# A mixer and mixture-of-experts layer on one core: the order of the weight loads, and which engine scales the transposed tokens

## The chip, the cores and the metric

The kernel runs on one core of a Trainium2 chip. The metric is the device time of one execution in microseconds (us), as the median of three runs. All arithmetic is float32. TensorE (PE in the profile) multiplies matrices, VectorE (DVE), ScalarE (ACT) and GpSimd (POOL) work on rows of 128 partitions, and SyncE (SP) issues nearly all loads in the order of one program of its own, here called the SP queue.

## What is computed

One layer for 256 latent tokens and 256 context tokens of width 1024, cut to what matters here:

```python
mod_x = silu(c) @ w_mod + b_mod            # w_mod (1024, 6144): shift1, scale1, gate1, shift2, scale2, gate2
hx = modulate(rmsnorm(x, g_mix), x_sh1, x_sc1)      # the same for the context, with c_ctx
ux = hx @ w_in; uc = hc @ w_in[:, POOL_W:]
ssm_x = ssm_output(ux_ssm, scans...)       # two directions, 32 groups of 64 complex states, GELU, sigmoid GLU
pool_x = pool_mixer(ux[..., :POOL_W], w_pool, s_pool)
x = x + x_g1 * (concatenate([pool_x, ssm_x]) @ w_out)
hx2 = modulate(rmsnorm(x, g_ffn), x_sh2, x_sc2)
eidx, gate = route(hx2, w_router, b_router)         # 2 of 32 experts for each token
for each expert e:                         # w_gate, w_up (1024, 512), w_down (512, 1024)
    y += gate * ((silu(h @ w_gate[e]) * (h @ w_up[e])) @ w_down[e])
return rmsnorm(x + x_g2 * y, g_final)
```

## The kernel before

The program of each engine is written out by hand, with semaphores between them; nothing reorders it. A load of 128 x 2048 float32 is 1 MiB; w_mod comes as 24 such chunks, a third (8 chunks, k = 0 to 7) for each pair of the six vectors.

**The head.** Tokens are normalised by ScalarE and transposed by TensorE (L456), four 128 x 128 pieces for each k of the 8 column blocks, into two PSUM banks in turn. Whoever empties a bank applies scale and shift in the same step and writes hT: ScalarE for even k (L851), VectorE for odd k (L1112, in `modulate_tokens`, which `powers_times` calls in the middle of its last products for SA). TensorE may fill a bank again when it has been emptied (semaphores `ht_ready`, `ht_ready_dve`). Behind it come the second half of the transposes of SA (L435, `turn_sa`), the projection u (L484, L491), the states' matmuls (L528), and VectorE's scans, which end with `hp_ready`.

The last third of w_mod isn't multiplied on TensorE: VectorE sums its chunks, weighted, into `acc` (`mod_sum`, L1237 and L1240), chunks 0 to 2 right behind the scans, 3 to 5 behind `ysum` (L1251), 6 and 7 behind the products that fill `cat` (L1257, printed as L999, the line of the helper `tt`). The chunks go through three buffers; the SP queue asks for chunk k of this third when VectorE has counted up `mod2_used` to k - 2. `y_mm` tells that L591 is done, `mix_pool` that the pooling part of the output projection is. TensorE's L610 is the matmul of the GLU, ScalarE's L916 its sigmoid, L621 the second part of the output projection, four blocks of four matmuls; before its third block stands L628, which turns `acc` into a column and waits for all eight chunks (`mod2_used`).

**The expert rounds.** Eight rounds (`four`) of four experts j = 0 to 3. For each expert TensorE multiplies gate and up side by side (`gate_up`, L728 and L729), each in two halves of k, 2 MiB a half, and counts `gu_half` behind each half. There are two buffers for gate and up, b = j % 2, and four for down, one for each expert. Behind the four experts and the adding of the round before (`scatter`, L702) come the down matmuls of all four experts, side by side in four column groups (`down`, L761), again in two halves; `down_half` is counted after the first half, `down_mm` at the end. Then `gather` (L696) lays out the tokens of the next round. The SP queue asks for a half when its buffer is free: `second_two(i)` loads gate and up of j = 2, 3 of round i, `downs(i)` the down matrices of round i, `next_two(i)` gate and up of j = 0, 1 of round i + 1. Round 0's down matrices are loaded in the head.

TensorE matmuls of float32 are two instructions each in the profile, transposes one.

The functions that the diff touches follow, with the lines of the profile.

Of the kernel before, what the change touches and what calls it, by code (L numbers as in the profile page):

```python
# [6 lines left out]
ALU = mybir.AluOpType  # L7
# [50 lines left out]
def hybrid_block(nc, x, ctx, w_mod, columns, ssm_bc, b_mod_rows, w_in, w_out, w_pool, w_glu, w_router, b_router,  # L58
                 w_gate, w_up, w_down, g_final, consts, pool_consts, out):
    D = x.shape[2]  # L60
    KD = D // P
    T = x.shape[1]
    NT = T // P
    NE = w_router.shape[1]
# [8 lines left out]
    with ExitStack() as stack:  # L73
# [164 lines left out]
        def _(sp):  # L238
# [53 lines left out]

            sp.wait_ge(S("mix_pool"), 1)
            sp.wait_ge(S("hp_ready"), 1)
            gu_load(sp, 0, 0, 0, "up")
            gu_load(sp, 0, 0, 1, "up")
            for half in range(2):
                down_load(sp, lambda j: j, half, (0, 1))

# [3 lines left out]
            for k in range(3, KD):  # L303
                mod_chunk(2, k)
            sp.wait_ge(S("mod2_used"), KD)
# [17 lines left out]
            def downs(i):  # L323

                sp.wait_ge(S("down_half"), i)
                down_load(sp, lambda j: (4 * i + j) % NE, 0)
                sp.wait_ge(S("down_mm"), 4 * i)
                down_load(sp, lambda j: (4 * i + j) % NE, 1)
# [12 lines left out]
            with sp.Fori(1, last_four) as i:  # L341
                second_two(i)
                downs(i)
                next_two(i)
            second_two(last_four)
            downs(last_four)
            for t in range(2 * NT):
                sp.wait_ge(S("fin_ready"), t + 1)
                tt, h = t // 2, t % 2
# [52 lines left out]
        def _(pe):  # L402
# [22 lines left out]
            def turn_sa(d, r):  # L425

                pe.wait_ge(S("sa_ready"), 2 * d + r + 1)
                for g4 in range(4):
                    n = 8 * d + 4 * r + g4
                    if n in (8, 9):  # L430
                        pe.wait_ge(S("ht_ready_dve" if n % 2 else "ht_ready"), KD)
                    elif n >= 2:
                        pe.wait_ge(S("st_copy"), n - 1)
                    for g in range(4):
                        mm = pe.transpose(ps[:, (n + 1) % 2, 128 * g:128 * g + 128],  # L435
                                          SA[:, d, r, 4 * g4 + g].rearrange("p s j -> p (s j)"), ident)
                    mm.then_inc(S("sa_t"), 1)
# [12 lines left out]
            for k in range(KD):  # L450
                if k == 1:
                    pe.wait_ge(S("mod_col"), 1)
                elif k >= 2:
                    pe.wait_ge(S("ht_ready_dve" if k % 2 else "ht_ready"), 2 * (k // 2))
                for t in range(4):
                    mm = pe.transpose(ps[:, (k + 1) % 2, 128 * t:128 * t + 128], xc[:, t, P * k:P * k + P], ident)  # L456
                mm.then_inc(S("x_t"), 1)
# [37 lines left out]
            pe.wait_ge(S("ht_ready"), KD)  # L495
            pe.wait_ge(S("ht_ready_dve"), KD)
# [306 lines left out]
        def _(act):  # L803
# [44 lines left out]
            for k in range(0, KD, 2):  # L848
# [140 lines left out]
        def _(dve):  # L989
# [85 lines left out]
            def powers_times(dst, pw, m, r, sign_im, done, between=None):  # L1075

                for d in range(2):
                    for rr in r:
                        for h in range(2):
                            if between and (d, rr, h) == (1, 1, 1):  # L1080
                                between()
# [24 lines left out]
            def modulate_tokens():  # L1106

                dve.wait_ge(S("a1_ready"), 1)
                for k in range(1, KD, 2):
                    dve.wait_ge(S("x_t"), k + 1)  # L1110
                    for q in (1, 0):
                        dve.tensor_scalar(hT[:, k, 256 * (1 - q):256 * (2 - q)], ps[:, (k + 1) % 2, 256 * (1 - q):256 * (2 - q)],  # L1112
                                          A1[:, k, q:q + 1], MC[:, 0, k, q:q + 1], ALU.mult, ALU.add).then_inc(S("ht_ready_dve"), 1)

            powers_times(SA, PW, Br, (0, 1), 1, "sa_ready", modulate_tokens)


# [341 lines left out]
```

## Time and profile before

| | |
|---|---|
| median of three runs | 716.72 us (716.46 to 719.92) |
| profiled execution, its own time | 720.47 us |
| its span, first to last instruction | 718.7 us |
| mean granted TensorE clock | 0.943 |
| busy: PE, DVE, ACT, POOL | 602.8, 217.3, 144.3, 23.8 us |
| loaded by the SP queue (q1) | 244.98 MB |
| mean rate of all loads | 344 GB/s |

Times of the trace are microseconds from the first instruction. In the page's rows a digit or a number stands for a fortieth of the span. A row of the windows gives the stretch, its length, the busy time of PE, PEld (TensorE's weight loads), DVE, ACT and POOL with the number of instructions in brackets, the mean granted TensorE clock (1.00 is 2.4 GHz, 0.50 is 1.2 GHz), the busy share of the 16 DMA engines and the rate in GB/s. A row of the chain of waits gives start, duration, and what was worked on or waited for; a row of the timeline gives start, duration, engine, line, operation, written tile <- read tiles, their sizes, and in brackets how long the engine was idle before and what ended that. SPq is the SP queue issuing a load; the load itself runs later. The name "ra" covers the tokens, hT and the expert inputs, "rc" the last two down buffers and SA, "wts" the weight buffers and cat, "r" is the third w_mod buffer.

### The profile page before, as it was taken

The numbers are of one execution on the slowest core, as the hardware profiler recorded it, in microseconds if no ns is written. First come the engines' busy times: TensorE is split into PE (matmuls) and PEld (weight loads), VectorE is DVE, ScalarE is ACT, GpSimd is POOL, SyncE is SP. The second block draws the span as 40 slices with busy tenths as digits, with TensorE's granted clock in tenths as the row PEclk, the third lists the DMA queues.
The fourth block names the chain that finished last, engine by engine and source line by source line (L and its number), as shares of the span: only waits on it lengthen the run. The fifth ranks groups of instructions, "written<-read, shape, count | busy, mean of one in ns | idle before, by whom it ended". The sixth has DMA issues, their size and how long they took to land.

```text
span 718.7 us, 9339 instructions
## 1 busy us (share of the span) xinstructions
PE 602.8 (84%) x3784; PEld 259.8 (36%) x3784; DVE 217.3 (30%) x494; ACT 144.3 (20%) x224; POOL 23.8 (3%) x31
## 2 busy tenths in 40 slices
PE   4658997887496999997998898899799889889875
PEld 0236436445242433432433333243343333334221
DVE  7974974992756200200200200010020020010003
ACT  3632014203011221221221221022122112102011
POOL 1800000000000000000000000000000000000000
PEclk9778999996798999999999999999999999999998
DMA  8981447789647699399999999999999999999981
GB/s 343 407 322 30 133 76 231 247 340 420 262 176 310 255 423 387 138 425 423 420 423 423 421 422 422 422 421 421 423 421 423 422 422 422 422 422 420 421 342 58
DMA packets 44078, 247.26 MB, mean 344 GB/s; under 512 B 8356, under 2 KB 10036, under 8 KB 16280
## 3 DMA queue, kind: packets, MB, share of 16 engines
q1 hardware_dynamic: 39592, 244.98, 84.4%
q10 hardware_dynamic: 4160, 1.05, 0.6%
q0 software_dynamic: 304, 0.93, 0.4%
q8 instruction: 15, 0.25, 0.1%
q14 instruction: 7, 0.06, 0.0%
HBM read 242.75 MB, written 2.10 MB: 341 GB/s over the span
## 4 chain that ended last, share of the span: by engine, by line
PE 34%; DMA 31%; SPq 6%; DVE 4%; issue 2%; ACT 1%; POOL 0%; DVEq 0%; ACTq 0%; POOLq 0%
DMA rc<-in_w_down 26%; PE ps L728 16%; PE ps L761 10%; SPq L233 5%; PE ps L696 4%; DMA wts<-in_w_mod 3%; DMA wts<-in_w_up 2%; PE ps L621 1%; SPq L226 1%; PE ps L702 1%; PE ps L591 1%; DVE ra L999 1%; DVE cb L999 0%; DVE rc L999 0%; DVE ra L1276 0%
## 5 line engine op out<-in xcount | busy, mean ns | idle before, releaser
L728 PE MATMUL ps<-wts,ra 128*64 128x512 f32 x512 | 227.0, 595 | 17.7 <-DMA wts<-in_w_up 16.3
L729 PE MATMUL ps<-wts,ra 128*64 128x512 f32 x512 | 227.2, 596 | 0.0
L761 PE MATMUL ps<-wts,ra 128*32 128x512 f32 x512 | 119.3, 621 | 31.0 <-DMA rc<-in_w_down 31.0
L728 PEld LDWEIGHTS ps<-wts,ra 128*64 128x64 f32 x512 | 67.2, 137 | 156.4 <-issue 126.6
L761 PE MATMUL ps<-rc,ra 128*32 128x512 f32 x512 | 119.3, 622 | 0.0
L999 DVE TENSOR_TENSOR ra<-ra,ps 128x256 f32<-128x256 f32 x32 | 13.5, 421 | 264.7 <-ACT ra L956 264.6
L950 ACT COPY ra<-ps 128x512 f32<-128x512 f32 x32 | 33.6, 1050 | 199.7 <-PE ps L729 199.7
L761 PEld LDWEIGHTS ps<-wts,ra 128*32 128x32 f32 x512 | 32.5, 114 | 109.2 <-issue 83.5
L729 PEld LDWEIGHTS ps<-wts,ra 128*64 128x64 f32 x512 | 67.2, 137 | 0.0
L999 DVE TENSOR_TENSOR cb<-ps,ra 128x512 f32<-128x512 f32 x32 | 22.1, 692 | 142.9 <-PE ps L761 142.9
L945 ACT COPY ra<-ps 128x512 f32<-128x512 f32 x32 | 18.4, 587 | 148.8 <-PE ps L696 141.9
L696 PE MATMUL ps<-cb,ra 128*128 128x128 f32 x256 | 32.6, 288 | 1.5 <-issue 1.2
L696 PEld LDWEIGHTS ps<-cb,ra 128*128 128x128 f32 x256 | 30.9, 201 | 7.6 <-DVE cb L999 5.9
L702 PE MATMUL ps<-cb 128*128 128x512 f32 x68 | 32.9, 606 | 0.0
L761 PEld LDWEIGHTS ps<-rc,ra 128*32 128x32 f32 x512 | 29.6, 114 | 0.0
L484 PE MATMUL ps<-ra,wts 128*128 128x512 f32 x64 | 29.1, 608 | 0.0
L621 PE MATMUL ps<-wts 128*128 128x512 f32 x32 | 17.4, 703 | 9.0 <-DVE wts L999 9.0
L414 PE MATMUL ps<-wts,sil 128*32 128x512 f32 x88 | 15.2, 770 | 8.9 <-DMA wts<-in_w_mod 8.9
L739 PEld LDWEIGHTS ps<-cst,ra 128*128 128x128 f32 x128 | 14.2, 140 | 17.2 <-issue 15.3
L999 DVE TENSOR_TENSOR ps<-pws,cb 128x1024 f32<-128x1024 f32 x16 | 20.2, 1264 | 0.0
L398 POOL TENSOR_TENSOR small<-small 128x1 f32<-128x1 f32 x4 | 2.2, 555 | 538.4 <-DVE small L1406 496.1
L999 DVE TENSOR_TENSOR rc<-pws,cb 128x1024 f32<-128x1024 f32 x16 | 19.6, 1224 | 0.6
(218 smaller groups left out, 515.9 us busy)
## 6 DMA issues: line engine op xcount, KB each, us to landing
wts<-in_w_up SPq DMA_DIRECT2D x64, 1024.0 KB, 13.2
wts<-in_w_gate SPq DMA_DIRECT2D x64, 1024.0 KB, 11.1
wts<-in_w_down SPq DMA_DIRECT2D x32, 1024.0 KB, 18.2
rc<-in_w_down SPq DMA_DIRECT2D x32, 1024.0 KB, 22.3
wts<-in_w_mod SPq DMA_DIRECT2D x16, 1024.0 KB, 10.0
r<-in_w_mod SPq DMA_DIRECT2D x8, 1024.0 KB, 11.2
wts<-in_w_in SPq DMA_DIRECT2D x2, 2048.0 KB, 14.0
wts<-in_w_out SPq DMA_DIRECT2D x2, 2048.0 KB, 10.4
```

Of the source, the lines that this page charges most:

```text
L233: eng.dma_start(Wd[j].rearrange("p k d -> p (k d)")[:, at], w_down[0, four(j)].rearrange("(p k) d -> p (k d)", k=FC)[:, at]).then_inc(S(f" ...
L414: mm = pe.matmul(ps[32 * j:32 * j + 32, bank, :], silc[:, k, :], wm[n % 3][:, 512 * j:512 * j + 512], start=False, stop=(k == KD - 1))
L484: mm = pe.matmul(ps[:, 4 + q % 3, :], WB[:, k, 512 + P * q:512 + P * q + P], hT[:, k, :], start=(k == 0), stop=(k == KD - 1))
L621: mm = pe.matmul(ps[:, n, :], cat[:, 4 + k, P * (n // 2):P * (n // 2) + P], wo_ssm[:, k, 512 * (n % 2):512 * (n % 2) + 512], start=False, ...
L696: mm = pe.matmul(o, h2P[:, t, k, :], Pm[:, t], start=True, stop=True, skip_group_check=True)
L702: mm = pe.matmul(ps[:, 2 * t + h, :], PT[:, t, :], oS[:, 2 * h + t, :], start=False, stop=stop, skip_group_check=True)
L728: pe.matmul(ps[0:64, 4 + b, :], st, Wg[b][:, k, :], start=(k == 0), stop=(k == KD - 1))
L729: mm = pe.matmul(ps[64:128, 4 + b, :], st, Wu[b][:, k, :], start=(k == 0), stop=(k == KD - 1))
L761: mm = pe.matmul(ps[32 * j:32 * j + 32, BANKS[n], :], hid[:, j, f, SLOTS * t:SLOTS * t + SLOTS], Wd[j][:, f, 512 * h:512 * h + 512], start ...
L945: act.copy(xm[:, 2 * r:2 * r + 2], ps[:, BANKS[r], :].rearrange("p (k e s) -> p k e s", k=2, e=4)).then_inc(S("xm_ready"), 1)
L950: act.copy(gu[:, j % 2, :].rearrange("p (f q) -> p q f", f=FC), ps[:, 4 + j % 2, :].rearrange("p (q f) -> p q f", f=FC)).then_inc(S("gu_co ...
L999: return dve.tensor_tensor(o, a, b, op)
```

## The change

The SP queue's order changes at two places. In the head, chunks 3 to 5 of w_mod's last third move ahead of everything else, the x rows ahead of the two up loads, and the down loads of experts 0 and 1 behind chunks 6 and 7. In the rounds, `downs` is split into halves, and both are asked for ahead of `second_two(i)`; in the last round only the first half is, and the second one stays behind. And ScalarE scales all eight k of the transposed tokens; VectorE's part of it and the semaphore `ht_ready_dve` are gone, so that `ht_ready` counts to 16.

```diff
--- before.py
+++ after.py
@@ -290,18 +290,19 @@
             for k in range(3):
                 mod_chunk(2, k)
 
+            for k in range(3, 6):
+                mod_chunk(2, k)
             sp.wait_ge(S("mix_pool"), 1)
             sp.wait_ge(S("hp_ready"), 1)
-            gu_load(sp, 0, 0, 0, "up")
-            gu_load(sp, 0, 0, 1, "up")
-            for half in range(2):
-                down_load(sp, lambda j: j, half, (0, 1))
-
             sp.wait_ge(S("y_mm"), 1)
             for t in range(NT):
                 sp.dma_start(x2[:, t, :], x[0, t * P:(t + 1) * P]).then_inc(S(f"xres_in{t}"), 16)
-            for k in range(3, KD):
+            gu_load(sp, 0, 0, 0, "up")
+            gu_load(sp, 0, 0, 1, "up")
+            for k in range(6, KD):
                 mod_chunk(2, k)
+            for half in range(2):
+                down_load(sp, lambda j: j, half, (0, 1))
             sp.wait_ge(S("mod2_used"), KD)
             gu_load(sp, 0, 0, 0, "gate")
             gu_load(sp, 0, 0, 1, "gate")
@@ -320,12 +321,10 @@
                         sp.wait_ge(S("gu_half"), 8 * i + 2 * b + half + 1)
                         gu_load(sp, b, (4 * i + 2 + b) % NE, half)
 
-            def downs(i):
-
-                sp.wait_ge(S("down_half"), i)
-                down_load(sp, lambda j: (4 * i + j) % NE, 0)
-                sp.wait_ge(S("down_mm"), 4 * i)
-                down_load(sp, lambda j: (4 * i + j) % NE, 1)
+            def downs(i, half):
+
+                sp.wait_ge(S("down_mm" if half else "down_half"), 4 * i if half else i)
+                down_load(sp, lambda j: (4 * i + j) % NE, half)
 
             def next_two(i):
 
@@ -339,11 +338,13 @@
             sp.wait_ge(S("passes_ready"), 1)
             last_four = sp.value_load(pairs[0:1, 0:1], min_val=NE // 4 - 1, max_val=NE - 1)
             with sp.Fori(1, last_four) as i:
+                downs(i, 0)
+                downs(i, 1)
                 second_two(i)
-                downs(i)
                 next_two(i)
+            downs(last_four, 0)
             second_two(last_four)
-            downs(last_four)
+            downs(last_four, 1)
             for t in range(2 * NT):
                 sp.wait_ge(S("fin_ready"), t + 1)
                 tt, h = t // 2, t % 2
@@ -428,7 +429,7 @@
                 for g4 in range(4):
                     n = 8 * d + 4 * r + g4
                     if n in (8, 9):
-                        pe.wait_ge(S("ht_ready_dve" if n % 2 else "ht_ready"), KD)
+                        pe.wait_ge(S("ht_ready"), 2 * KD)
                     elif n >= 2:
                         pe.wait_ge(S("st_copy"), n - 1)
                     for g in range(4):
@@ -451,7 +452,7 @@
                 if k == 1:
                     pe.wait_ge(S("mod_col"), 1)
                 elif k >= 2:
-                    pe.wait_ge(S("ht_ready_dve" if k % 2 else "ht_ready"), 2 * (k // 2))
+                    pe.wait_ge(S("ht_ready"), 2 * (k - 1))
                 for t in range(4):
                     mm = pe.transpose(ps[:, (k + 1) % 2, 128 * t:128 * t + 128], xc[:, t, P * k:P * k + P], ident)
                 mm.then_inc(S("x_t"), 1)
@@ -492,8 +493,7 @@
                                    start=(k == 0), stop=(k == KD - 1))
                 mm.then_inc(S("u_pool_mm"), 1)
 
-            pe.wait_ge(S("ht_ready"), KD)
-            pe.wait_ge(S("ht_ready_dve"), KD)
+            pe.wait_ge(S("ht_ready"), 2 * KD)
             pe.wait_ge(S("win_ssm_in"), 16)
             turn_sa(1, 0)
             u_ssm(0)
@@ -845,7 +845,7 @@
             mod_columns(0, 0)
 
             act.wait_ge(S("a1_ready"), 1)
-            for k in range(0, KD, 2):
+            for k in range(KD):
                 act.wait_ge(S("x_t"), k + 1)
                 for q in (1, 0):
                     act.activation(hT[:, k, 256 * (1 - q):256 * (2 - q)], ps[:, (k + 1) % 2, 256 * (1 - q):256 * (2 - q)],
@@ -1072,13 +1072,11 @@
                 link(tt(bi_, bi_, u, ALU.add))
             dve.sem_inc(S("bbar_ready"), 1)
 
-            def powers_times(dst, pw, m, r, sign_im, done, between=None):
+            def powers_times(dst, pw, m, r, sign_im, done):
 
                 for d in range(2):
                     for rr in r:
                         for h in range(2):
-                            if between and (d, rr, h) == (1, 1, 1):
-                                between()
                             g = slice(8 * h, 8 * h + 8)
                             pr = pw[:, d, 0, g].unsqueeze(3).broadcast_to([P, 8, L, SG])
                             pi = pw[:, d, 1, g].unsqueeze(3).broadcast_to([P, 8, L, SG])
@@ -1103,16 +1101,7 @@
                         ins.then_inc(S(done), 1)
                         dve.wait_ge(S(done), 2 * d + rr + 1)
 
-            def modulate_tokens():
-
-                dve.wait_ge(S("a1_ready"), 1)
-                for k in range(1, KD, 2):
-                    dve.wait_ge(S("x_t"), k + 1)
-                    for q in (1, 0):
-                        dve.tensor_scalar(hT[:, k, 256 * (1 - q):256 * (2 - q)], ps[:, (k + 1) % 2, 256 * (1 - q):256 * (2 - q)],
-                                          A1[:, k, q:q + 1], MC[:, 0, k, q:q + 1], ALU.mult, ALU.add).then_inc(S("ht_ready_dve"), 1)
-
-            powers_times(SA, PW, Br, (0, 1), 1, "sa_ready", modulate_tokens)
+            powers_times(SA, PW, Br, (0, 1), 1, "sa_ready")
 
 
             dve.wait_ge(S("x_t"), KD)
```

The rows of the SP queue in the head, from behind the third chunk of w_mod's last third. wts and r<-in_w_mod are its chunks, rc<-in_x the x rows, L226 and L233 the lines that load gate or up, and down. Before:

```order
L226 DMA wts<-in_w_up 128x2048 [waits hp_ready,mix_pool]
L226 DMA wts<-in_w_up 128x2048
L233 DMA wts<-in_w_down 128x2048 x4
L302 DMA rc<-in_x 128x1024 [waits y_mm]
L302 DMA rc<-in_x 128x1024
L252 DMA wts<-in_w_mod 128x2048 [waits mod2_used]
L252 DMA r<-in_w_mod 128x2048 [waits mod2_used]
L252 DMA wts<-in_w_mod 128x2048 [waits mod2_used] x2
L252 DMA r<-in_w_mod 128x2048 [waits mod2_used]
```

And now:

```order
L252 DMA wts<-in_w_mod 128x2048 [waits mod2_used]
L252 DMA r<-in_w_mod 128x2048 [waits mod2_used]
L252 DMA wts<-in_w_mod 128x2048 [waits mod2_used]
L299 DMA rc<-in_x 128x1024 [waits y_mm,hp_ready,mix_pool]
L299 DMA rc<-in_x 128x1024
L226 DMA wts<-in_w_up 128x2048 x2
L252 DMA wts<-in_w_mod 128x2048 [waits mod2_used]
L252 DMA r<-in_w_mod 128x2048 [waits mod2_used]
L233 DMA wts<-in_w_down 128x2048 x4
```

Three of the five chunks stand ahead of all expert weights, the other two behind the up loads and ahead of the down loads.

The same queue from the start of its loop over the rounds 1 to 6 (the branch). Before, the loop starts with the gate and up loads of `second_two`:

```order
L341 UNCONDITIONAL_BRANCH
L341 ISA
L226 ISA [waits gu_half]
L226 DMA wts<-in_w_gate 128x2048
L226 DMA wts<-in_w_up 128x2048
L320 REGISTER_ALU
L226 ISA [waits gu_half]
L226 DMA wts<-in_w_gate 128x2048
L226 DMA wts<-in_w_up 128x2048
```

And now with the down loads:

```order
L340 UNCONDITIONAL_BRANCH
L233 ISA [waits down_half]
L233 DMA wts<-in_w_down 128x2048
L233 ISA
L233 DMA wts<-in_w_down 128x2048
L233 ISA
L233 DMA rc<-in_w_down 128x2048
L233 ISA
L233 DMA rc<-in_w_down 128x2048
L233 ISA [waits down_mm]
```

The second half of the down loads, with its wait for `down_mm`, follows there, and only then the eight loads of `second_two`.

## Rows read from the trace of the kernel before

**Rows 1.** Page, part 2: GB/s moved in 40 slices of 17.97 us.

```profile
GB/s 343 407 322 30 133 76 231 247 340 420 262 176 310 255 423 387 138 425 423 420 423 423 421 422 422 422 421 421 423 421 423 422 422 422 422 422 420 421 342 58
```

**Rows 2.** Windows: us, busy us per engine, TensorE clock, DMA share, GB/s.

```profile
265.00:286.00 21.00, 19.78 (x136) 7.08 (x136) 0.84 (x2) 2.18 (x4) 0.00 (x0) 1.00 1.01 418
286.00:299.50 13.50, 13.50 (x102) 6.61 (x92) 3.86 (x7) 3.62 (x5) 0.00 (x0) 1.00 0.07 16
299.50:399.50 100.00, 89.43 (x508) 33.49 (x504) 7.24 (x15) 18.09 (x25) 0.00 (x0) 0.98 1.01 421
599.50:697.30 97.80, 85.40 (x496) 32.36 (x492) 6.90 (x14) 14.27 (x23) 0.00 (x0) 1.00 1.01 420
```

**Rows 3.** Chain of waits, its last links: start us, us, what.

```profile
672.32 26.89 DMA rc<-in_w_down
699.25 8.51 PE ps L761 x64
```

**Rows 4.** Chain of waits between 160 and 205 us.

```profile
167.03 20.75 DMA wts<-in_w_mod
...
190.84 10.17 PE ps L621 x16
```

**Rows 5.** Timeline 158 to 198 us: start, us, engine, line, tiles, idle before.

```profile
158.80 0.80 SPq L226 DMA_DIRECT2D wts<-in_w_up  x2
158.82 1.29 DVE L1237 TENSOR_SCALAR cb<-wts,sil 128x2048 f32<-128x2048 f32 x1
159.65 2.35 SPq L233 DMA_DIRECT2D wts<-in_w_down  x4
...
166.08 0.43 SPq L252 DMA_DIRECT2D wts<-in_w_mod  x1
...
171.07 1.66 DVE L1251 SCALAR_TENSOR_TENSOR rc<-ut,vt,ps 128x256 f32<-128x256 f32 x4 [6.02 <-PE ps L601]
...
181.00 1.70 ACT L916 ACTIVATE rc<-ps,vt 128x256 f32<-128x256 f32 x4 [6.53 <-PE ps L610]
182.87 2.35 DVE L1240 SCALAR_TENSOR_TENSOR cb<-wts,sil,cb 128x2048 f32<-128x2048 f32 x1 [10.15 <-DMA wts<-in_w_mod]
...
190.08 2.02 DVE L999 TENSOR_TENSOR wts<-rc 128x256 f32<-128x256 f32 x4
```

**Rows 6.** Timeline 39 to 56 us, the transposed tokens.

```profile
39.70 1.02 ACT L851 ACTIVATE ra<-ps,mcol,aux 128x256 f32<-128x256 f32 x2 [1.36 <-POOL aux L382]
...
44.26 0.99 DVE L1112 TENSOR_SCALAR ra<-ps,aux,mcol 128x256 f32<-128x256 f32 x2
...
49.73 1.12 PE L456 MATMUL ps<-cst,ra 128*128 128x128 f32 x4 [0.22 <-DVE ra L1112]
...
51.98 3.78 PE L435 MATMUL ps<-cst,rc 128*128 128x128 f32 x16 [1.14 <-DVE ra L1112]
```

**Rows 7.** Windows around the transposes of rows 6, columns as in rows 2.

```profile
47.50:50.00 2.50, 2.26 (x10) 1.70 (x11) 1.00 (x2) 1.29 (x3) 0.00 (x0) 0.50 0.98 410
...
55.50:58.00 2.50, 2.50 (x6) 1.11 (x5) 2.33 (x20) 0.62 (x2) 0.76 (x1) 0.68 0.33 84
```

**Rows 8.** Chain of waits, 235 to 300 us: TensorE through the first round.

```profile
240.94 0.64 PE ps L728
...
268.08 0.64 PE ps L728
...
276.46 13.87 PE ps L761 x128
290.33 3.77 PE ps L696 x32
```

**Rows 9.** Timeline of the SP queue, 290 to 300 us.

```profile
297.95 0.35 SPq L226 DMA_DIRECT2D wts<-in_w_gate  x1
```

**Rows 10.** Windows of the third round, columns as in rows 2.

```profile
337.50:340.00 2.50, 0.03 (x3) 0.00 (x0) 0.00 (x0) 0.00 (x0) 0.00 (x0) 1.00 1.01 419
340.00:342.50 2.50, 2.20 (x12) 0.61 (x16) 0.00 (x0) 0.00 (x0) 0.00 (x0) 0.58 1.01 419
...
377.50:380.00 2.50, 1.31 (x7) 0.17 (x3) 0.00 (x0) 0.00 (x0) 0.00 (x0) 1.00 1.02 423
```

## Prediction

> **What bounds the kernel now.** I read the rate of the loads first. From slice 18 on they move 420 to 425 GB/s in every slice [rows 1], and the windows show the same 421 GB/s over 100 us at a stretch [rows 2]: the expert rounds are bound by the loads. One round loads 24 MiB (four experts of three 2 MiB matrices), 25.2 MB, so it lasts 59.8 us at 421 GB/s, while TensorE needs less: in the first round, with its matrices mostly there, it goes from 240.94 us to 294.10 us (290.33 + 3.77), 53.2 us [rows 8]. What the time is made of is then the head until the round starts, any hole in the stream of loads, and the tail behind the last byte.
>
> There is one hole in the expert rounds: 16 GB/s between 286.0 and 299.5 us [rows 2]. The first round asks for 16 MiB of gate and up matrices and then nothing, because the SP queue first wants the second round's gate and up matrices, for which TensorE must have used the first ones of that round. It does that from 294.10 us, and the request comes at 297.95 us [rows 8, 9]. The stream is full again at 299.5, so a request takes 1.5 us to reach the wires.
>
> The tail is 1.95 us from the last byte (697.3 us, [rows 2]) to the matmul that waited for it (699.25 us), and 8.51 us of the last 64 down matmuls [rows 3].
>
> In the head, the chain of waits has 20.75 us of a w_mod load and then the output projection on TensorE, L621 [rows 4]. The timeline says why: two up loads and four down loads, 6 MiB, are asked for at 158.80 us, and the fourth w_mod chunk of the last third only at 166.08 us, behind them; VectorE is idle for 10.15 us and sums it at 182.87. The products for the output projection stand behind three such sums on VectorE: they start at 190.08, though their sigmoids exist from about 181.5 us [rows 5].
>
> **The tokens, ScalarE alone.** Now VectorE comes late to its first column (44.26 us, it was in the middle of the SA products), and TensorE's transposes end so that the next step starts at 51.98 us [rows 6]. ScalarE alone does one k in 1.02 us (two halves), so eight end 8.16 us after 39.70, at 47.9, if the transposes keep up with two PSUM banks. At the lower clock four of them take 1.12 us [rows 6]; with about 0.1 us of hand-over on top of 1.02 + 1.12, a pair of k takes 2.25 us instead of 2.04, and six k so add 0.6 us. L435 starts at 48.6: **3.4 us earlier**. VectorE loses its eight scalings, 4 x 1.0 us, and the waits between them, and is ready earlier than it is wanted. ScalarE's own queue holds only the copies of the transposed SA behind this, which wait for TensorE anyway. Everything up to 158 us hangs on TensorE and then on VectorE's scans, so I carry the 3.4 us on whole.
>
> One thing can make it more. The clock was at half (0.50, its 1.2 GHz level) from 47.5 to 50 us although TensorE was busy 2.26 of 2.50 us with transposes, and it rose only in the window from 55.5, where the matmuls of u begin [rows 7]. So I keep it at half for the longer run of transposes as well. If it stayed at full, the hand-over would cost nothing (0.6), L435's 3.78 us would be 1.9 shorter at most, and this term 5.9 at most. The Trainium skill (TensorE: Matmul & The Clock Gate, Part 4: PE-mode transpose) says that a transpose does not count as work for the clock gate; by that rule the term is 3.4, which is what I sum, and by busy time alone it would be up to 5.9.
>
> **w_mod ahead of the expert weights.** Chunks 3, 4 and 5 are asked for as soon as VectorE has used chunks 0, 1 and 2, at about 160, 163 and 165 us of the old time, on a nearly empty queue. Each is 2.5 us of stream; so they are there before VectorE is through with ysum at 172.7 (171.07 + 1.66). Three sums of 2.35 us plus the gaps then end at 180.1, before the first sigmoid is done at 181.5. The products start there instead of at 190.08: **8.5 us earlier** [rows 5]. What is moved behind: the x rows, asked for after chunk 5 (about where they were), the two up loads, then chunks 6 and 7, which wait for the fourth and fifth sum (175.1 and 177.6). Ahead of chunk 6 stand chunks 3 to 5, 1 MiB of x and 2 MiB of up; that ends at 176.6, so chunk 7 is through at 181.6 and lands near 183.6. The sums 6 and 7 run after the products, from 183.6 to 188.4. TensorE wants them after eight matmuls of L621 (16 passes), started at 182.3. So they are just in time. The down loads of experts 0 and 1 end about 192 us and are needed 80 us later: nothing.
>
> L621's 16 passes took 10.17 us [rows 4] behind 9 us in which TensorE waited. Now they follow L610 within 1 us. In the rounds a pass takes 0.43 us at full clock (13.87 us for 32 steps of four matmuls side by side, [rows 8]), so 7.0 us: **3.2 us**. The first round so starts 3.4 + 8.5 + 3.2 = 15.1 us earlier, at 225.8.
>
> **Down matrices first.** The first half of the next round's down matrices is asked for when TensorE is half through this round's down matmuls: 276.46 + 6.9 = 283.4 us [rows 8], 2.6 us before the stream ran dry at 286.0. With 1.5 us to reach the wires there are 1.1 us to spare, and the hole closes: **13.5 us**.
>
> Then each round. Let F be the last byte of a round's gate and up matrices. TensorE starts on it 1.95 us later, is at the down matmuls 8.4 us after that (268.08 to 276.46), half through after another 6.9 [rows 8], and the request reaches the wires at F + 18.8. Meanwhile the queue holds the next 8 MiB, to F + 19.9. That is again 1.1 us to spare. Behind it all is loose: the second half is asked for at F + 24.2 and due at F + 28.4, the gate and up matrices at F + 31.8 and due at F + 38.3. So the waits added to the SP queue hold nothing up. For ragged hand-overs I take 0.2 us at each of seven requests, **1.4 us lost**; the ends are 0, and 2 us each, if the request comes 3 us later than I worked out.
>
> **The tail.** In the last round the second half of the down matrices comes last, behind the gate and up matrices. The queue holds 8 MiB and the first half, to F + 29.9. The next load needs TensorE to have used the first gate and up half of the last round: 1.95 + 8.4 + 13.87 + 3.77 + 3.85 (294.10 to 297.95) = F + 31.8, on the wires at F + 33.3: a new hole of 3.4 us. 8 MiB end at F + 53.2, and TensorE then does the last gate and up half, the turns and all 128 down matmuls: 1.95 + 8.4 + 13.87 = 24.2, F + 77.4. The old order would end at F + 59.8 + 1.95 + 8.51 = F + 70.2. **7.2 us lost**.
>
> **Sum.** 15.1 + 13.5 - 1.4 - 7.2 = 20.0 us. The profiled execution took 720.47 us, so it becomes 700.5; the median of the runs is 3.75 us lower than that execution, 716.72, and becomes **696.7 us**.
>
> **Rivals.** (1) *The down request comes too late in every round.* It has 1.1 us to spare and decides the stream. Landing by landing the matmuls ahead of it (L728, L702, L739) may wait for the last gate and up half a little longer. At 1 to 2 us lost in each of seven rounds, the time is 702 to 709. For it: the small margin. Against it: the first round's durations come from one trace without a gap on TensorE.
> (2) *The sums 6 and 7 are late.* They have under 1 us against TensorE's wait before L628. If chunk 7 lands 5 us later, the time is 702. Against it: nothing but 7 MiB is ahead of it after 160 us.
> (3) *Slower: the clock.* TensorE now idles before the third expert of each round, from F + 42 to F + 46.7, and a wait of under 3 us was enough to put the clock at 0.58 in the next 2.5 us [rows 10]. The four halves that follow are paced by loads of 5.0 us and cost it 3.4 us each, or 6.9 at half clock. If the clock stayed low through them and through the first half of the down matmuls, the request would come 6.9 us later, 5.8 us past the end of the queue, seven times: 41 us, so 737. It decides from 4.2 us of delay a round on (3.1 us times 7 eat the gain). Against it: with TensorE busy 1.31 of 2.50 us, in waits of the same kind, the clock stayed at 1.00 [rows 10].
> The Trainium skill (TensorE: Matmul & The Clock Gate, HAM oscillation) describes kernels that fall back to half clock at each wait for a load; by that rule this rival would hold in every round.
>
> **Chances.** Forecast 0.72, rival 1 0.14, rival 2 0.08, rival 3 0.06. A difference of 0.5%, 3.6 us, is about what a measurement of this kernel can tell. The first three are faster by more than that; of the third rival I count 0.02 as no change and 0.04 as slower. Faster 0.94. For the range: the lower end takes the full clock at the transposes (2.5), no ragged hand-overs (1.4) and a smaller tail (the new hole of 3.4 may close), down to 690; the upper end takes in most of rival 1 and rival 2, 706. Rival 3 and the rest of rival 1 are left out.
>
> **What would show it.** L851 sixteen times without VectorE's L1112, and L435 at 48 to 49 us; the products of L621 right behind the sigmoids; the first L728 near 226 us; no window under 400 GB/s from there to about 650; a DMA hole of some 3 us in the last round; from the last gate and up load 24 us to the end of the down matmuls, which wait for nothing. I am wrong if the stream has a hole in each round, if TensorE's clock is under 1.00 in the down matmuls, or if the first round starts later than 230 us.

## The result and the profile after

The changed kernel takes 696.92 us (median of 4 runs, 695.08 to 700.18), the kernel before in the same comparison 716.59 us (715.38 to 719.92): ratio 0.9712, 95% interval 0.9687 to 0.9737. In a second comparison, run for this study, it took 697.21 against 716.56 us, ratio 0.9737 (0.9708 to 0.9766). The forecast was 696.7 us, 20.0 us less; measured are 19.7 and 19.4 us less.

The profiled execution of the changed kernel took 696.92 us, exactly its median, with a span of 694.9 us; the one before had 720.47 and 718.7. From profile to profile the span is 23.8 us shorter, 4 us more than from median to median. Where these 4 us come from, as far as the runs tell, is part of what follows.

The rate of all loads after the change, in 40 slices of 17.37 us; the 138 of [rows 1] is gone, and a 342 has appeared in slice 37:

```profile
GB/s 342 384 395 32 140 108 262 238 309 394 421 277 241 344 422 421 423 422 420 423 422 422 420 423 422 422 422 423 421 420 421 422 421 423 423 421 342 423 243 61
```

Windows of the profile after, columns as in [rows 2]:

```profile
248.00:268.00 20.00, 18.77 (x124) 6.75 (x124) 0.84 (x2) 2.19 (x4) 0.00 (x0) 1.00 1.01 421
268.00:288.00 20.00, 20.00 (x136) 8.77 (x130) 3.86 (x7) 4.70 (x6) 0.00 (x0) 1.00 1.01 421
...
308.00:636.00 328.00, 299.50 (x1778) 114.81 (x1776) 32.10 (x63) 58.71 (x83) 0.00 (x0) 0.96 1.01 422
636.00:640.50 4.50, 4.50 (x24) 1.46 (x22) 0.00 (x0) 0.00 (x0) 0.00 (x0) 1.00 0.44 137
```

The stream runs at 421 to 422 GB/s through the place where the hole of 13.5 us was, and up to 636 us. The new hole, 4.5 us at 137 GB/s, is in the last round; at 422 GB/s it is worth 3.0 us. Its end, in the chain of waits after, which answers to [rows 3]:

```profile
649.89 11.84 DMA wts<-in_w_up
...
670.15 13.87 PE ps L761 x128
```

The last gate and up load lands at 661.73 us, and TensorE needs 22.3 us from there to the end of all 128 down matmuls at 684.02. The chain counts a load up to its landing, and that is later than its last byte: in [rows 3] the last down load lands at 699.21 us (672.32 + 26.89), 1.9 us behind the last byte at 697.3. From the last byte it is therefore about 24.2 us.

The head, timeline of the profile after, which answers to [rows 5] (L1226 and L1229 are VectorE's sums, L436, L485 and so on the lines that were one lower before):

```profile
151.88 5.17 PEld L591 LDWEIGHTS ps<-rc,ra 64*32 64x32 f32 x256 [4.01 <-DVE ra L999]
...
153.24 0.33 SPq L252 DMA_DIRECT2D wts<-in_w_mod  x1
...
165.68 2.35 DVE L1229 SCALAR_TENSOR_TENSOR cb<-wts,sil,cb 128x2048 f32<-128x2048 f32 x1
...
170.59 2.35 DVE L1229 SCALAR_TENSOR_TENSOR cb<-wts,sil,cb 128x2048 f32<-128x2048 f32 x1
...
174.27 1.70 ACT L916 ACTIVATE rc<-ps,vt 128x256 f32<-128x256 f32 x4 [6.75 <-PE ps L610]
174.78 2.02 DVE L999 TENSOR_TENSOR wts<-rc 128x256 f32<-128x256 f32 x4 [1.84 <-ACT rc L916]
...
175.55 7.11 PE L621 MATMUL ps<-wts 128*128 128x512 f32 x16 [0.45 <-DVE wts L999]
...
182.49 1.84 PE L628 MATMUL ps<-cst,cb 128*128 128x1 f32 x16
```

The w_mod chunk that was asked for at 166.08 us is asked for at 153.24, as soon as VectorE, through with its scans, has summed chunk 0 (151.93 to 153.22). Sum 3 runs at 165.68 right behind `ysum`, sum 5 is over at 172.94, and the products start with the sigmoids (174.78 behind 174.27). From L591 to L621 it is 23.67 us, where it was 32.06 (158.78 to 190.84, [rows 4]). The last sum ends at 181.41, and L628 starts at 182.49 without a wait.

The tokens, timeline of the profile after, and two windows; they answer to [rows 6, 7]:

```profile
39.73 7.40 ACT L851 ACTIVATE ra<-ps,mcol,aux 128x256 f32<-128x256 f32 x16 [1.48 <-POOL aux L383]
...
47.28 3.61 PE L436 MATMUL ps<-cst,rc 128*128 128x128 f32 x16 [1.26 <-ACT ra L851]
```

```profile
42.50:45.00 2.50, 1.86 (x12) 1.26 (x12) 2.43 (x3) 2.50 (x7) 0.00 (x0) 1.00 1.08 420
...
47.50:50.00 2.50, 2.50 (x12) 2.14 (x12) 2.33 (x18) 1.17 (x2) 0.76 (x1) 0.50 1.01 419
```

ScalarE does all sixteen halves in 7.40 us without a pause, and L436 starts at 47.28 instead of 51.98 us. The clock is at 1.00 in the middle of the transposes of the tokens and falls to half only behind them, in L436, which are transposes too.

### The profile page after: what moved, and what is told of

The parts are those of the page before. It is cut to its first block, busy times and chain, and to the rows that moved or that the text cites. A ratio compares the mean times of both kernels' runs of the same rounds, so it can differ in the third digit from the quotient of the medians.

```text
span 694.9 us, 9344 instructions
## 1 busy us (share of the span) xinstructions
PE 601.9 (87%) x3784; PEld 255.8 (37%) x3784; DVE 213.3 (31%) x486; ACT 147.7 (21%) x232; POOL 24.0 (3%) x31
## 4 chain that ended last, share of the span: by engine, by line
PE 52%; DMA 20%; DVE 2%; issue 2%; ACT 1%; SPq 0%; POOL 0%; DVEq 0%; ACTq 0%; POOLq 0%
DMA wts<-in_w_up 20%; PE ps L728 20%; PE ps L761 16%; PE ps L702 4%; PE ps L696 4%; PE ps L610 1%; PE ps L621 1%; PE ps L739 1%; PE ps L591 1%; DVE ra L999 1%; PE ps L641 1%; SPq L226 0%; PE ps L576 0%; DVE rc L999 0%; DVE ra L1265 0%
## 5 line engine op out<-in xcount | busy, mean ns | idle before, releaser
L728 PE MATMUL ps<-wts,ra 128*64 128x512 f32 x512 | 240.2, 624 | 37.3 <-DMA wts<-in_w_up 36.0
L729 PE MATMUL ps<-wts,ra 128*64 128x512 f32 x512 | 240.3, 625 | 0.0
L728 PEld LDWEIGHTS ps<-wts,ra 128*64 128x64 f32 x512 | 70.5, 143 | 186.5 <-issue 137.4
L761 PE MATMUL ps<-wts,ra 128*32 128x512 f32 x512 | 111.4, 593 | 0.0
L761 PE MATMUL ps<-rc,ra 128*32 128x512 f32 x512 | 111.4, 593 | 0.0
L999 DVE TENSOR_TENSOR ra<-ra,ps 128x256 f32<-128x256 f32 x32 | 13.5, 422 | 297.7 <-ACT ra L956 297.5
L729 PEld LDWEIGHTS ps<-wts,ra 128*64 128x64 f32 x512 | 70.5, 143 | 0.0
L761 PEld LDWEIGHTS ps<-wts,ra 128*32 128x32 f32 x512 | 29.2, 110 | 73.1 <-issue 73.1
L485 PE MATMUL ps<-ra,wts 128*128 128x512 f32 x64 | 28.3, 595 | 0.0
L739 PE MATMUL ps<-cst,ra 128*128 128x128 f32 x128 | 18.8, 280 | 0.0
## 6 DMA issues: line engine op xcount, KB each, us to landing
r<-in_w_mod SPq DMA_DIRECT2D x8, 1024.0 KB, 10.3
```

The source lines that it names most:

```text
L485: mm = pe.matmul(ps[:, 4 + q % 3, :], WB[:, k, 512 + P * q:512 + P * q + P], hT[:, k, :], start=(k == 0), stop=(k == KD - 1))
L728: pe.matmul(ps[0:64, 4 + b, :], st, Wg[b][:, k, :], start=(k == 0), stop=(k == KD - 1))
L729: mm = pe.matmul(ps[64:128, 4 + b, :], st, Wu[b][:, k, :], start=(k == 0), stop=(k == KD - 1))
L739: mm = pe.transpose(ps[:, 6 + j % 2, P * f:P * f + P], gu[:, j % 2, P * f:P * f + P], ident)
L761: mm = pe.matmul(ps[32 * j:32 * j + 32, BANKS[n], :], hid[:, j, f, SLOTS * t:SLOTS * t + SLOTS], Wd[j][:, f, 512 * h:512 * h + 512], start ...
L999: return dve.tensor_tensor(o, a, b, op)
```

## Experiments

Each kernel was timed against the kernel before in the same comparison, and profiled. Ratios are to the kernel before, with the 95% interval; microseconds less with a range behind them are worked out from the ratio, and differ by up to 1.3 us from the difference of the two medians. The three kernels with a single execution each are named where they come.

### Each part alone

Three kernels have one part of the change each, the rest as before: the diff's parts on `ht_ready` and `modulate_tokens`; its part in the head of the SP queue; its parts on `downs`. A fourth has the two new orders without the tokens' part.

**Tokens alone.**

> The kernel before with only the tokens scaled by ScalarE alone; both orders of loads as before. The two profiles differ by 6.9 us at the matmuls L591 (158.78 and 151.88 us), where I had worked out 3.4. If that is the part's doing, about 6.9 us less than before, 0.990; if the forecast's size was right and the rest came from how TensorE's clock fell in the two profiled executions, 3.4 us less, 0.995. Either way it passes to the end in full, because the stream of expert loads starts with the first round.

Measured: 713.14 against 718.48 us, ratio 0.9936 (0.9911 to 0.9962), 4.6 us less (2.7 to 6.4). The forecast's 3.4 lies in that range, the 6.9 between the two profiles does not.

**Order in the head alone.**

> The kernel before with only the new order in the head (w_mod chunks 3 to 5 first, down loads behind chunks 6 and 7). The forecast has 8.5 + 3.2 = 11.7 us less, 0.984: L621 right behind the sigmoids and 7.1 us long. The profile of the changed kernel gives 1.3 us back before the first round (18.35 us early at L652, 17.1 at the first L728); if that belongs to this part, 10.2 us less, 0.986. Rival: the products wait for something else (glu, clock) and it brings under 5 us.

Measured: 705.93 us, ratio 0.9823 (0.9779 to 0.9866), 12.7 us less (9.6 to 15.9). The forecast's 11.7 and the profile's 10.2 both lie in that; the rival's 5 does not.

**Down matrices first, alone.**

> The kernel before with only the down matrices asked for first in each round. Forecast: hole of 13.5 us closed, 7.2 lost in the tail, 1.4 at the requests: 4.9 us less, 0.993. With the sizes of the changed kernel's profile (tail 6.4, rounds nothing) it is 7.1 less, 0.990. Rival: the closed hole comes back as waits in each round, then nothing or slower.

Measured: 711.32 us, ratio 0.9903 (0.9877 to 0.9929), 7.0 us less (5.1 to 8.8). The 7.1 of the expectation lies in that range, and so do the 6.7 us by which the two profiles differ from the first L728 to the end of the down matmuls; the forecast's 4.9 is just outside.

**Both orders, without the tokens' part.**

> Both new orders of loads, tokens scaled by both engines as before. If the parts add up, it lies between the two kernels by what the tokens' part is worth: 690 + 10 = about 704 if that is 6.9, 700 if it is 3.4. If the tokens' gain is hidden behind loads once the orders are new, it is as fast as the changed kernel, 697.

Measured: 698.88 us, ratio 0.9745 (0.9708 to 0.9782), 18.3 us less (15.6 to 20.9). Within the intervals the two orders of loads add up: 12.7 + 7.0 = 19.7. What the tokens' part adds to them is not resolved: the changed kernel's ratios of 0.9712 and 0.9737 are 2.4 and 0.6 us below this one, each known to 2 us and this one to 2.6.

**The changed kernel once more.**

> The changed kernel as it is, on the same chip as the others and with more runs: ratio 0.971 as recorded. The parts alone gave 0.9936, 0.9823 and 0.9903, 24 us together, and the kernel with only the tokens' part undone 0.9745. If the parts add up exactly, 0.966 to 0.968; the tokens' part then is worth 4 to 5 us here too. If the tokens' part is hidden once the loads are reordered, 0.974.

Measured: 0.9737 (0.9708 to 0.9766). That is the number of the expectation's last case, the tokens' part hidden (0.974), and leaves out its first, 0.966 to 0.968; the first comparison's 0.9712 (0.9687 to 0.9737) stands between the two. The three parts alone make 24.3 us, with intervals that together come to about 4 us; the changed kernel gains 18.8 to 20.6 by its two ratios, 19.4 to 19.7 by the medians. So the sum of the parts is on the high side, and the shortfall is at the edge of what these runs can tell. That the tokens' part is worth something in the changed kernel too is argued from its profiles, and not shown by its times.

### The clock in the head

The profiles tell more than the times here. The start of L591, behind which both orders of loads first differ, and of the first L728, in us (the same code may print one line more or less):

| profile | tokens | head order | L591 | first L728 |
|---|---|---|---|---|
| before | both engines | old | 158.78 | 240.94 |
| before, second profile | both | old | 158.50 | 240.76 |
| downs alone | both | old | 154.30 | 236.30 |
| head order alone | both | new | 155.31 | 227.45 |
| both orders | both | new | 154.76 | 223.69 |
| tokens alone | ScalarE | old | 150.51 | 232.25 |
| after | ScalarE | new | 151.88 | 223.85 |
| after, second profile | ScalarE | new | 150.44 | 222.02 |

The second profile of the kernel before was made for this question.

> The kernel before, a second profile. In the profile that the prediction read, the clock was at half during L435 and the first matmuls of u (51.98 to 57 us) and during L467; in the profiles of three kernels with the same code up to there it was not, and L591 started 3.5 to 4.5 us earlier (154.3 to 155.3 instead of 158.78). If that is chance of the execution, this profile has L591 at 154 to 159 us and a span lower by as much as L591 is earlier; if it belongs to the kernel, 158.8 us again.

It has 158.50 us, and its execution took 720.28 us. So the late L591 is nothing odd in one profile: of five executions with this code two are 3.2 to 4.5 us later than the other three. In the two late ones the clock was at 0.50 from 45 us to the first matmuls of u and again in L467; in the other three L467 took 3.70 us instead of 5.3 to 5.4. The early ones had the same wait on TensorE (3.6 to 3.9 us, against 3.9), but a clock that came back while TensorE did nothing but transposes. The windows of the kernel with the downs alone:

```profile
45.00:47.50 2.50, 1.97 (x9) 1.57 (x10) 1.24 (x3) 0.39 (x1) 0.00 (x0) 0.61 1.02 426
47.50:50.00 2.50, 2.18 (x12) 1.66 (x11) 1.00 (x2) 1.40 (x4) 0.00 (x0) 0.71 1.01 419
50.00:52.50 2.50, 1.24 (x10) 0.85 (x8) 2.28 (x4) 0.72 (x2) 0.00 (x0) 1.00 0.23 95
```

The first matmul of u is at 53.65 us there. In [rows 7] the clock stayed at half through the same instructions.

The same happens again between L591 and the first L728. That stretch takes 72.14 us with the head order alone and 71.6 to 72.0 us in the two profiles of the changed kernel, but 68.93 us with both orders. About half of the 3.2 us lies where L601 stands (1.09 us with both orders, 1.97 in the other three), the rest behind a wait of 5.1 us on TensorE that all four have at about 200 us: with both orders the clock is at 1.00 again from 207.5 to 215 us, with the head order alone it stands at 0.50 until 212.5. So the profile with both orders reaches the first L728 as early as the changed kernel, although its L591 is 3 to 4 us later. From L591 on, the profiles show no wait that would swallow what the tokens' part gains: with the old head order it is 81.74 us for the tokens alone, against 82.00 to 82.26.

Two kernels lengthen that stretch, one with transposes and one with plain matmuls:

```diff
             turn_sa(1, 0)
+            for n in range(96):
+                pe.transpose(ps[:, 5, 0:128], ident, ident)
             u_ssm(0)
```

```diff
             turn_sa(1, 0)
+            for n in range(48):
+                pe.matmul(ps[:, 5, 0:128], ident, ident, start=True, stop=True)
             u_ssm(0)
```

> The changed kernel with 96 more transposes of the identity into an unused PSUM bank, between L436 and the first matmuls of u, where the clock stood at half (0.50 from 47.5 to 50 us); they change no result. If a transpose does not count as work for the clock, it stays at 0.50 through all of them, and they last about 21 us (0.22 each). If it counts by busy time, the clock is back at 1.00 within a few us and they last 13 to 15 us.

> The twin of the one with 96 transposes: 48 plain matmuls of 128 x 128 by 128 columns, each two passes, in the same place. They count as work by either rule: the clock should be at 1.00 within a few us of their start, and they last 13 to 17 us.

Timeline and windows of the kernel with 96 transposes more (L500):

```profile
49.68 10.64 PE L500 MATMUL ps<-cst 128*128 128x128 f32 x96
```

```profile
50.00:52.50 2.50, 2.50 (x25) 2.50 (x24) 2.29 (x20) 0.47 (x1) 0.00 (x0) 1.00 0.50 200
...
57.50:60.00 2.50, 2.50 (x25) 2.50 (x24) 0.00 (x0) 0.00 (x0) 0.00 (x0) 1.00 0.00 0
```

And of its twin with matmuls (L500 too):

```profile
48.31 3.79 PE L436 MATMUL ps<-cst,rc 128*128 128x128 f32 x16 [1.20 <-ACT ra L853]
51.89 11.26 PE L500 MATMUL ps<-cst 128*128 128x128 f32 x96
```

```profile
47.50:50.00 2.50, 1.69 (x8) 1.57 (x8) 2.33 (x16) 1.17 (x3) 0.76 (x1) 0.50 1.01 419
50.00:52.50 2.50, 2.50 (x13) 2.29 (x12) 2.33 (x20) 1.61 (x4) 0.00 (x0) 0.50 0.80 324
52.50:55.00 2.50, 2.50 (x24) 2.50 (x23) 2.29 (x20) 0.22 (x1) 0.00 (x0) 0.96 0.02 10
```

The 96 transposes took 10.64 us, 0.11 us each, at a clock of 1.00 from the first to the last window. That fits neither expectation as written, since in this execution the clock had not fallen at L436, and so it does not show that transposes can raise the clock. It shows that it can stay up under them: from the last matmul of w_mod's first third, which ends at 37 us, to the first of u at 60 us TensorE did nothing but transposes. They do not always keep it. With the same instructions up to L436 the clock fell to half in five of nine profiles with ScalarE alone: among the transposes of the tokens in the matmuls' twin and in the kernel with chunks 6 and 7 late, which is the last experiment below, and at L436 in the profile after and two more. The windows above, of the kernel with the downs alone, show a rise under transposes. In the matmuls' twin the clock stood at half from 42.5 us through the transposes up to 52 us, and was at 0.96 in the first whole window of the matmuls, as expected; these took 11.26 us, less than the 13 to 17 expected. The two kernels took 708.70 and 709.33 us, in one execution each. So under transposes alone the clock rose from half in three executions (the kernels with the downs alone, with the head order alone and with both orders: at 0.84 to 1.00 between 50 and 52.5 us, with the first matmul of u at 53.7 to 54.3) and did not rise in four others (both profiles of before, the matmuls' twin, and the kernel with chunks 6 and 7 late). What decides that stays open.

### How much room the request for the down matrices has

```diff
-                sp.wait_ge(S("down_mm" if half else "down_half"), 4 * i if half else i)
+                sp.wait_ge(S("down_mm"), 4 * i)
```

> The changed kernel, but both halves of the down matrices wait until TensorE is through with all down matmuls (down_mm), 6.9 us later than the first half is asked for now. My theory has 1.1 us to spare at that request, so each of seven requests opens a hole of 5.8 us: 41 us more, near 738, and the period of a round 65.4 us. If there is more room than I think (the queue holds more), it is less: with 5 us of room 13 us more. If the request is already late, up to 48 us more.

The requests in the SP queue of the changed kernel, one a round (the first, second, third and last round):

```profile
266.88 0.93 SPq L233 DMA_DIRECT2D wts<-in_w_down  x2
...
326.48 0.90 SPq L233 DMA_DIRECT2D wts<-in_w_down  x2
...
386.13 0.90 SPq L233 DMA_DIRECT2D wts<-in_w_down  x2
...
624.65 0.90 SPq L233 DMA_DIRECT2D wts<-in_w_down  x2
```

And with the later wait:

```profile
273.88 0.93 SPq L233 DMA_DIRECT2D wts<-in_w_down  x2
...
338.97 0.91 SPq L233 DMA_DIRECT2D wts<-in_w_down  x2
...
403.78 0.90 SPq L233 DMA_DIRECT2D wts<-in_w_down  x2
```

Measured: 732.69 us in one execution, against 697 us in other comparisons, so some 36 us more; the expectation was 41. The requests are 59.6 us apart in the changed kernel (and the down matmuls were 59.6 us apart before), 65.0 with the later wait. A delay of 6.8 to 7.0 us costs 5.4 us a round, so the request had about 1.5 us to spare, where I had worked out 1.1. Each round now has its hole, as in this window behind the first request's old place (the one of the next round is the same, 0 GB/s from 337 to 339 us):

```profile
272.00:274.00 2.00, 2.00 (x20) 0.73 (x13) 1.67 (x3) 0.00 (x0) 0.00 (x0) 1.00 0.00 0
```

This is the rival "the down request comes too late", made real: by this one point, were it 1.5 us later than it is, every microsecond more would cost seven.

### The tail

Two kernels move the down loads of the last round alone:

```diff
             downs(last_four, 0)
+            downs(last_four, 1)
             second_two(last_four)
-            downs(last_four, 1)
```

```diff
-            downs(last_four, 0)
             second_two(last_four)
+            downs(last_four, 0)
             downs(last_four, 1)
```

> The changed kernel, but in the last round both halves of the down matrices ahead of its last gate and up matrices. This closes the hole of about 3 us in the last round's loads. My theory: the end is set by the last gate and up matrices and 22 us of TensorE behind them; they now land 6.5 us later, so the time is about 6.5 us longer, 703 to 704. Rival: the hole is what the tail costs; then it is 3 us faster, 694.

> The changed kernel, but in the last round both halves of the down matrices behind its gate and up matrices, as before the change. The hole ahead of these becomes 13 us, but they are asked for and land at the same time as now. My theory: only the second half of the down matrices, landing 10 us later, is late for TensorE, by 5 us, so 702 to 704. Rival: the hole counts, 10 us more, 707.

Measured: both first 702.35 us, ratio 0.9793 (0.9765 to 0.9821), 5.1 us more than the changed kernel's 697.21 in the same comparison, where 6.5 were expected; both behind 703.78 us, 0.9816 (0.9784 to 0.9848), 6.6 us more, in the expected range. The chain of waits with both first:

```profile
649.34 19.17 DMA wts<-in_w_up
...
676.93 13.87 PE ps L761 x128
```

And with both behind:

```profile
654.12 27.83 DMA rc<-in_w_down
...
681.99 8.65 PE ps L761 x64
```

With both first the stream has no hole, and the kernel is slower all the same: the last gate and up load lands at 668.51 us, and 22.3 us of TensorE follow it to 690.80 us. The stream's last byte is at about 666.8 us there (298 GB/s from 665 to 667.5 us, nothing behind), 24.0 us before that end. With both behind, the end hangs on a down load that lands at 681.95. The rival, that the hole is what the tail costs, falls in both: closing it doesn't help, and ten more microseconds of it cost less than seven. The order of the changed kernel is the best of the three.

### Chunks 6 and 7 behind the down loads

```diff
-            for k in range(6, KD):
-                mod_chunk(2, k)
             for half in range(2):
                 down_load(sp, lambda j: j, half, (0, 1))
+            for k in range(6, KD):
+                mod_chunk(2, k)
```

> The changed kernel with the down loads of experts 0 and 1 ahead of w_mod chunks 6 and 7 instead of behind. These 4 MiB are 10 us of loads; chunk 6 then lands at about 184.5, chunk 7 at 187 to 189, VectorE's last sum ends near 191.5 instead of 181.4, and TensorE waits before L628 for it. Theory: 8 to 9 us more than the changed kernel, 705 to 706. Rival: the sums 6 and 7 have room; then the same time.

Measured: 707.48 us, ratio 0.986 (0.9827 to 0.9894), 10.3 us more than the changed kernel by the medians and 8.8 by the ratios, where 8 to 9 were expected. TensorE waits for the sum before L628 (the row has 14 of its 16 matmuls):

```profile
193.11 3.15 PE L628 MATMUL ps<-cst,cb 128*128 128x1 f32 x14 [7.28 <-DVE cb L1229]
```

L628 starts 14.4 us behind L621 instead of 6.9, and the idle wait also puts the clock at half for L628 (3.58 us for all 16 instead of 1.84): from L591 to the first L728 it is 81.89 us instead of 71.97, 9.9 us more. So the place of these two chunks matters, and the forecast's "just in time" is right: 1.1 us of room in the profile after.

## Why the prediction was right, step by step

The time, the sign and the reasons hold; that the time came out to 0.2 us is in part luck, as told below. The steps:

- **What bounds it** holds. The stream of loads sets the rounds at 59.6 us each, and what is gained ahead of the first round arrives at the end.
- **Tokens, 3.4 us:** too small. Two steps of it were mis-sized. I took 1.02 us for a k, two halves with the end of the second; back to back they take 0.93 (7.40 us for sixteen). And I added 0.6 us because the clock would be at half in the loop; it was at 1.00 up to 45 us. L436 was then 4.7 us early instead of 3.4. In the two profiles where the clock did fall among these transposes, L436 starts at 48.31 and 48.36 us, near the 48.6 of the forecast, so its figure fits the case that it assumed. Over all profiles with each head (five before, and seven with ScalarE alone: 150.4 to 155.1) L591 is at 156.3 us before and 152.0 now, 4.3 us; the part alone measured 4.6 us (2.7 to 6.4), but on top of the two orders it is not resolved. The Trainium skill's rule (TensorE: Matmul & The Clock Gate, Part 4: PE-mode transpose), that transposes do not count for the clock, does not hold as it stands: it agrees with the four executions in which the clock stayed at half under them, but not with the three in which it rose, nor with a run of 10.6 us of nothing else at 1.00. The range of this term, up to 5.9 us, was right to take that in.
- **w_mod, 8.5 us:** measured 8.4 (32.06 to 23.67 us from L591 to L621). **L621 at full clock, 3.2 us:** measured 3.1 (10.17 to 7.11).
- **First round 15.1 us earlier:** 17.1 between the two profiles, and by the table's means and the three other profiles of the new head with ScalarE alone (223.85, 223.61, 224.04; the one with chunks 6 and 7 late left out) 239.3 to 223.5, 15.8. In the profile after 18.35 us had been gained at L628, and 1.3 were given back: the clock was at 0.50 in the windows from 202.5 to 210 us, where before it was at 0.50 only from 217.5 to 222.5 us.
- **Hole of 13.5 us:** closed. **Requests, 1.4 us lost:** nothing, the rounds are 59.6 us apart before and after. **Tail, 7.2 us lost:** from the first L728 to the end of the down matmuls it is 466.82 us before and 460.17 after, 6.7 less, so tail and the rest together cost 6.9 us, where the forecast had 8.6. Of these 1.7 us, 1.4 are the requests and 0.4 the new hole, worth 3.0 us instead of 3.4; the 24.2 us from the last byte to the end of the down matmuls came out (the 22.3 of the chain start at the landing).
- **The profiled execution** is where the sum came out right by luck in part. I made the sum against 720.47 us and carried it over to the median by a fixed 3.75 us. That execution was one of those in which the clock was low at 45 to 57 us and in L467, while the profiled execution after is the median of its runs. From profile to profile the span fell by 23.8 us, 3.8 more than the 20.0 of the sum: 2.0 of them lie ahead of the first round (17.1 against 15.1) and 1.8 behind it (6.7 against 4.9). The 3.75 us that I took off took this up almost exactly, and nothing in my working said that it would. How much of the 3.8 us is the change and how much the chance of two executions is not resolved; the late L591 of the profile before (158.78 us, against a mean of 156.3) accounts for up to 2.5.
- **Rival 1** (request too late) did not happen, with 1.5 us of room. **Rival 2** (sums 6 and 7 late) did not happen, with 1.1 us of room. **Rival 3** (the clock) happened as far as I had it and no further. Windows of the profile after, third round:

```profile
352.50:355.00 2.50, 0.00 (x0) 0.00 (x0) 0.42 (x1) 1.02 (x2) 0.00 (x0) 0.88 1.01 419
355.00:357.50 2.50, 1.92 (x6) 0.69 (x8) 0.00 (x0) 0.00 (x0) 0.00 (x0) 0.50 1.01 419
...
362.50:365.00 2.50, 2.50 (x14) 0.70 (x10) 0.00 (x0) 0.00 (x0) 0.00 (x0) 1.00 1.01 419
...
385.00:387.50 2.50, 2.50 (x32) 0.73 (x24) 0.00 (x0) 0.00 (x0) 0.00 (x0) 1.00 1.01 419
```

TensorE idles 4.2 us before the third expert of a round, in the slot forecast, and goes on at 0.50 for about 5.5 us, into the window from 360 to 362.5 us; L728's mean is 624 ns instead of 595. The gate and up loads that pace it then hide this, and the clock is back at 1.00 long before the down matmuls. The rule of the Trainium skill that a wait for a load puts the clock back (the same page, HAM oscillation) agrees with this: it fell in this wait and cost nothing, since the load was the slower one. It did not fall in every wait for a load: the next one, of 0.9 us at 369.6 us, left it at 1.00.

## What to carry to other kernels

When one queue of loads sets the pace, look for the request in it that waits for the engine longest, and put requests that are already free ahead of it; then work out by how much each request comes before the queue runs dry, because that margin, here about 1.5 us of a 59.6 us round, is what the order stands on. In the last round the measure changes: what counts there is the landing of the load with the most work behind it, and a hole ahead of it may be harmless. Before a sum is made against a single profile, see whether its time stands at the median of its runs, and if it doesn't, find the stretch that differs first.

## What the runs showed that I had not expected

- Two executions of the same code differ by 3 to 4 us through TensorE's clock alone. In the head of the kernel before, L591 starts at 154.3 to 155.3 us in three profiles and at 158.5 and 158.8 in two; two kernels with the same head, one with the head order alone and one with both orders, reach the first L728 at 227.45 and 223.69 us, most of it by the clock between L591 and there.
- In one execution TensorE did nothing but transposes for over 20 us and the clock stayed at 1.00; in three executions it rose from half under transposes alone, in four others it did not.
- An idle wait on TensorE costs more than its length where matmuls follow that somebody waits for: 7.3 us before L628 made L628 1.7 us longer, and came to 9.9 us of delay by the first round.
